# Last attention of a two-block transformer kernel: turning, scoring and weighing each placed one weight unit later

## The reference, cut to what matters

```
h = rms_norm_2(x, att_norm)
q, k, v, g = split(h @ att_w_in)             # 2048 x 8192 weights, fp32
q = partial_rope(rms_norm_2(q)); k = partial_rope(rms_norm_2(k))   # 8 heads, 2 maps each, 128 wide
for each head:                               # diff_attention
    p[0], p[1] = softmax(causal(q[m] @ k[m].T * scale))   for m = 0, 1
    o = (p[0] - lam * p[1]) @ v
o = rms_norm_2(o) * (1 - lam_init) * silu(g)
x = x + o @ att_w_out
```

## Time and profile before

| | |
|---|---|
| median of 3 runs | 3389.58 us (3389.53 to 3390.03) |
| the profiled execution's own time | 3386.4 us |
| its span, first to last instruction | 3384.6 us |
| PE busy | 3317.2 us, 98% |
| DVE, ACT, POOL busy | 68%, 51%, 11% |
| mean granted TensorE clock | 0.997 |
| HBM traffic | 175 GB/s over the span |

### The profile page before, as it was taken

The page is one execution under the profiler, slowest core; times in us unless marked ns, Lnnn a source line. Parts: engine busy times, 40 slices in busy tenths (PEclk is TensorE's granted clock), DMA queues, the critical chain, the costliest instruction groups (busy, mean ns, idle before and its releaser), DMA issues.

```text
span 3384.6 us, 56343 instructions
## 1 busy us (share of the span) xinstructions
PE 3317.2 (98%) x18614; PEld 2866.3 (85%) x18614; DVE 2285.4 (68%) x3419; ACT 1714.9 (51%) x2500; POOL 379.8 (11%) x422
## 2 busy tenths in 40 slices
PE   8999999999999998999999999999999999999999
PEld 7888888887788877888888888888888888888888
DVE  6666666676656866665665677787666668656566
ACT  5444444454544655444444456774444444555554
POOL 1000000010022311000000001220242422100000
PEclk9999999999999999999999999999999999999999
DMA  7566566664544554666666655556544445555555
GB/s 227 186 199 187 185 192 186 188 190 144 160 147 148 193 155 138 187 190 187 187 191 187 185 181 176 189 178 188 162 149 149 149 149 164 184 162 180 169 168 166
DMA packets 236026, 592.48 MB, mean 175 GB/s; under 512 B 18832, under 2 KB 113296, under 8 KB 235808
## 3 DMA queue, kind: packets, MB, share of 16 engines
q1 hardware_dynamic: 234784, 587.12, 56.1%
q10 hardware_dynamic: 1152, 4.19, 0.3%
HBM read 589.14 MB, written 2.10 MB: 175 GB/s over the span
## 4 chain that ended last, share of the span: by engine, by line
PE 52%; issue 10%; DVE 3%; ACT 1%; POOL 1%; ACTq 0%; POOLq 0%
PE bank L495 31%; PE bank L494 8%; PE bank L497 8%; PE bank L733 2%; DVE w_low L1462 1%; PE bank L747 1%; POOL root_qk L2160 1%; ACT w_high L995 1%; DVE normed L1507 0%; PE bank L534 0%; PE bank L536 0%; PE bank L535 0%; DVE residual L1497 0%; PE bank L591 0%; PE bank L584 0%
## 5 line engine op out<-in xcount | busy, mean ns | idle before, releaser
L1462 DVE TENSOR_TENSOR w_low<-w_raw,w_high 128x1024 fp32r<-128x1024 f32 (+1 forms) x1120 | 1371.7, 1233 | 586.7 <-ACT w_high L995 567.8
L495 PE MATMUL bank<-normed,w_high 128*128 128x512 f32 x4800 | 1548.8, 399 | 14.6 <-DVE w_low L1462 10.3
L995 ACT ACTIVATE w_high<-w_raw 128x1024 fp32r<-128x1024 f32 (+1 forms) x1120 | 1165.8, 1044 | 696.0 <-PE bank L495 473.0
L495 PE MATMUL bank<-mixed,w_high 128*128 128x512 f32 x2496 | 794.2, 397 | 4.3 <-DVE increment L1494 4.3
L495 PEld LDWEIGHTS bank<-normed,w_high 128*128 128x128 f32 x4800 | 744.1, 189 | 17.9 <-issue 12.0
L494 PE MATMUL bank<-normed,w_low 128*128 128x256 f32 x2400 | 670.2, 279 | 0.0
L497 PE MATMUL bank<-normed,w_low 128*128 128x256 f32 x2400 | 667.3, 278 | 0.0
L494 PEld LDWEIGHTS bank<-normed,w_low 128*128 128x128 f32 x2400 | 451.9, 188 | 109.6
L497 PEld LDWEIGHTS bank<-normed,w_low 128*128 128x128 f32 x2400 | 453.1, 189 | 100.5 <-issue 1.7
L1012 ACT ACTIVATE parts<-bank 128x256 f32<-128x256 f32 x432 | 165.1, 382 | 689.3 <-PE bank L495 689.1
L495 PEld LDWEIGHTS bank<-mixed,w_high 128*128 128x128 f32 x2496 | 383.2, 189 | 7.0 <-issue 4.1
(11 more groups left out here) (288 smaller groups left out, 2367.5 us busy)
## 6 DMA issues: line engine op xcount, KB each, us to landing
w_raw<-w_hg SPq DMA_DIRECT2D x128, 512.0 KB, 3.6
w_raw<-w_att SPq DMA_DIRECT2D x128, 512.0 KB, 3.6
w_raw<-w_up1a SPq DMA_DIRECT2D x64, 512.0 KB, 4.2
w_raw<-w_up1b SPq DMA_DIRECT2D x64, 512.0 KB, 4.0
w_raw<-w_up2a SPq DMA_DIRECT2D x64, 512.0 KB, 4.2
w_raw<-w_up2b SPq DMA_DIRECT2D x64, 512.0 KB, 4.2
w_raw<-w_rg SPq DMA_DIRECT2D x64, 512.0 KB, 4.2
w_raw<-w_up1c SPq DMA_DIRECT2D x48, 512.0 KB, 4.0
```

The lines of the kernel that those rows point to most:

```text
L495: last = nc.tensor.matmul(banks[b][:, :], hi, x, start=starts and k == 0, stop=stop)
L995: A_(wh[slot][:, 0:width], raw[slot][:, 0:width], ACT.Copy).then_inc(wh_done, 1)
L1462: TT(wl[slot][:, 0:width], raw[slot][:, 0:width], wh[slot][:, 0:width].bitcast(F32), ALU.subtract).then_inc(wl_done, 1)
```

## The change

In the last attention `face` moves from slot 12 to 13 and `score` from slot 14 to 15 of the head itself, and `weigh` from slot 0 to slot 1 of the next head, on PE, ACT and DVE alike. `values` stays in slot 0, `turn` in slot 3, and `scale` in slot 11. No instruction is added or removed in the program as it executes.

```
-        AT_D = {0: [("values", 1), ("weigh", 1)], 3: [("turn", 1)], 5: [("mix", 1)], 6: [("norm", 1)],
+        AT_D = {0: [("values", 1)], 1: [("weigh", 1)], 3: [("turn", 1)], 5: [("mix", 1)], 6: [("norm", 1)],
                 8: [("gate", 1), ("rope0", 0), ("rope1", 0)], 9: [("sum", 0)], 10: [("oturn", 1)], 11: [("scale", 0), ("store", 1)],
-                12: [("face", 0)], 14: [("score", 0)]}
+                13: [("face", 0)], 15: [("score", 0)]}
```

## The result

The changed kernel takes 3406.48 us (median of 6 runs, 3404.15 to 3407.93), the kernel before 3389.72 (6 runs, 3389.53 to 3390.15): ratio 1.0049, interval 1.0037 to 1.0061. It is 16.8 us slower. The forecast was 3401.3 with a range of 3396 to 3407. The direction, the place and the wait were as forecast. The size came out 5 us above the forecast and just inside the range.

A forecast was written before the change was run, and what follows sets the result against it. PE, busy 98% of the span, was taken as the bound, so only its waits count: 7 x 2.5 + 2.4 - 8.2 = +11.7 us, moving the 3389.58 median to 3401.3 us, range 3396 to 3407.

The forecast's parts named there:

- The old wait: PE's wait for the scaled keys at slot 12, 1.08 us in seven heads, 0.65 in head 0; all 8.2 us go.
- S + 7.00 for the exponentials: With S the start of the score's matmuls, the exponentials should end 7.00 us later, as before the change.
- the walk through ACT's and DVE's queues: Program-order walk with old durations: weighing queued behind values and one more split, ending 14.69 us after the score's start.
- A pause of 2.5 us in each head: PE waits for the weighing at the turn of the probabilities, slot 3 of heads 1 to 7, 2.5 us each.
- the cushion: 2.95 us between the weighing's end and PE's turn of the probabilities in the kernel before; the change draws on it.
- The last head, +2.4 us: Going into the projection, waits of 2.14 for add_to_x, 0.35 at the turn, 0.28 behind, less the old 0.36.
- No further wait: Later splits, the mix, raw buffers and the programs of SP and POOL were expected to make nobody wait.
- The sum, +11.7: Net change over the last attention and projection: 7 x 2.5 + 2.4 - 8.2 = +11.7 us.
- PE's clock falls: Rival: half clock for 3.4 us after each of eight pauses, 1.7 us each, 13.6 us more, 3414.9 us; chance 0.05.
- The counterexample: PE's wait of 2.96 us at 1234.32, followed by a clock of 1.00, cited against a fall of the clock.
- the weighing in time: Rival: the turn of the probabilities does not wait, only the 8.2 us gain counts, 3381.4 us; chance 0.06.
- the table load off the path: Rival: silu's table load leaves ACT's path, weighing 1.28 us sooner, stall 1.2 a head, 3391 us; chance 0.04.

The follow-up runs named there:

- e1: The kernel before with only the turn of queries and keys (face) moved, from slot 12 to 13: 3379.41 us, ratio 0.9975.
- e2: The changed kernel with the weighing back in slot 0 of the next head: 3381.39 us, ratio 0.9980 to the kernel before.
- e3: The kernel before with only the weighing moved, from slot 0 to slot 1 of the next head: 3393.49 us, ratio 1.0017.
- e4: The changed kernel with values moved from slot 0 to slot 1, the weighing staying in slot 1: 3381.83 us, ratio 0.9983 to the kernel before.
- e5: The changed kernel with ten extra matmuls on PE before its wait for the weighing, heads 1 to 7: 3400.91 us, ratio 1.0035 to the kernel before.
- e6: The changed kernel with the weighing in slot 2 instead of slot 1: 3424.00 us, ratio 1.0104 to the kernel before.
- e7: The changed kernel with the turn of the probabilities in slot 4 instead of 3: 3381.87 us, ratio 0.9982 to the kernel before.

## Why the prediction was right, and where its size was short

- **The old wait goes.** Right, and e1 shows it alone. The term was 8.2 us; e1 gives 8.8, since PE also restarted 0.1 us slower behind each of these waits.
- **S + 7.00 for the exponentials, and the walk through ACT's and DVE's queues.** Right to 0.01 us in head 2.
- **A pause of 2.5 us in each head.** Right: 2.50 to 2.51 in six heads, 2.57 in the first. The prediction gave two reasons, 2.72 for the later score and 2.68 for the weighing's new place. As a sum they hold, but the two moves made alone don't cost that. The score alone takes 2.72 - 1.13 = 1.6 of the cushion and is harmless (e2), as it also leaves one split behind. The weighing alone takes 3.6 and uses up the cushion (e3). Put on top of e2 the weighing's move takes 14.69 - 10.88 = 3.81, and 3.81 - 1.13 is the prediction's 2.68. The lateness comes through ACT's values ahead of split 20's first half (e4).
- **The last head, +2.4 us.** Right: 2.14 at the third unit as forecast, 0.59 - 0.23 = 0.36 at the turn against 0.35, and 0.2 behind it against 0.28 (3316.72 is the next start, due at 3316.29 + 0.24). Less the old 0.36 that is 2.3.
- **No further wait.** Right, none is in PE's waits.
- **The sum, +11.7.** Right for the waits: e5, in which the turn is as late and only the clock doesn't fall, measures +11.9.
- **The rival "PE's clock falls" at a chance of 0.05.** This is the step that failed, by size. The prediction set it aside because one wait of 2.96 us was followed by a clock of 1.00, and because PE is otherwise full there. In fact it happened behind four of the seven pauses, in both profiled executions, at 1.5 to 1.6 us each, which makes (17.7 - 11.7) / 4 = 1.5 and the 6 us that this stage took beyond the forecast. It priced a fall about rightly (1.7 us) and treated it as all or none: eight falls would have given 3414.9, none 3401.3, and four at 1.5 give 3407.3, against a median of 3406.5. The six executions scatter the same way: their mean granted clock is 0.993 in the three slowest (3406.72 to 3407.93) and 0.995 in the fastest (3404.15). That the median still lay inside the range owes something to luck: the range was widened for small errors of the walk, and e6 shows falls behind six of seven pauses.
- **The counterexample itself was one draw.** The same wait on the same work is in all ten profiled executions, 2.96 us each time. In eight of them no fall follows it, and in e5 and e6, where the program is the same up to there, one does. In e5 (line 913 is line 910 of the others), a timeline row and then a stretch as in the earlier trace rows:

```profile
1234.06 1.12 PE L913 MATMUL bank<-diag,ones 128*128 128x512 f32 x2 [2.96 <-DVE squares L1937]
```

```profile
1235.10:1238.50 3.40, 3.40 (x9) 2.08 (x8) 0.78 (x2) 0.00 (x0) 0.00 (x0) 0.50 0.48 154
```

At the 3.88 us wait of the earlier trace rows the clock fell in all ten.
- **The rivals on the other side** (the weighing in time, the table load off the path) did not occur. In the first of them the bound "split 20 behind it by S + 12.2" is a slip: the whole weighing has to be done by then, so the split would have to be done by S + 10.5, and the 2.45 us named there is right. In e4 ACT gets to that split before values, which takes 2.67 us off the weighing's end, and the pause is gone. The silu's table load is 1.28 us as before (3052.59) and the next activation follows at once (3053.88), so the drain that the Trainium skill (ScalarE: Activation LUTs, What ACT_TABLE_LOAD costs) adds behind it did not show in this kernel either.

## What to carry to other kernels

When a step is moved later in a table that several in-order engines share, work out its arrival from what is queued ahead of it on each engine, and compare with the cushion of the step that does not move; here moving one step of the chain gained 8.6 us, and moving three lost 17. Of a pause on PE count two prices: the pause, and a chance of a fall of the clock behind it, which one counterexample doesn't remove. Count what followed the same wait in several executions before giving that chance a number. The best version found is e1, 3379.4 us, 0.25% faster than the kernel before.

## What the runs showed of the hardware that was not expected

Behind pauses of 2.5 us in an otherwise full PE the granted clock fell to 0.50 for 3.4 us four times of seven in each of two executions, at a cost of 1.5 to 1.6 us each, and behind 3.7 us six times of seven (e6), twice for 6.8 us. Behind the projection's pause of 2.1 us (the changed kernel in both executions, e2, e5, e6, e7) it fell in none of six, and behind pauses of 0.7 and 1.1 us (e3) it never fell in this stage. Length alone doesn't decide it: the wait of 2.96 us near 1234 was followed by a fall in two of ten executions, fewer than the pauses of 2.5 us. The Trainium skill (TensorE: Matmul & The Clock Gate, Part 1) describes a clock that falls when the array has been less active; the runs agree, and filling the pause with matmuls kept it up (e5). Which of equal pauses is followed by a fall differed between two executions of one program, and why it differed stays open.
